# The shared expert's products and the first two expert passes in another order, in a mixture-of-experts layer

## The reference, cut to what matters

```python
def swiglu(t, wg, wu, wd):
    return (jax.nn.silu(t @ wg) * (t @ wu)) @ wd

def moe_ffn(h, ...):                       # T = 512 tokens, D = 1024
    scores = jax.nn.sigmoid(t @ w_router)  # 64 experts, group-limited top 8
    ...                                    # tokens sorted by expert, blocks of one expert
    def expert_block(args):
        tok, wb, e = args
        yb = swiglu(t_pad[tok], w_e_gate[e], w_e_up[e], w_e_down[e])
        return yb * wb[:, None]
    routed = jax.ops.segment_sum(...)      # added back to the tokens' rows
    shared = swiglu(t, w_sh_gate, w_sh_up, w_sh_down)
    return routed + shared
```

## Time and profile before

| | us |
|---|---|
| median of 3 runs | 1037.86 |
| lowest and highest | 1037.82, 1041.65 |
| the profiled execution | 1042.4 |
| its span | 1040.6 |
| TensorE busy in it | 944.7 (91%) |
| DVE, ACT, POOL busy | 513.2, 330.9, 400.1 |
| mean granted TensorE clock | 0.964 |

### The profile page before, as it was taken

The page is one execution under the profiler, slowest core; times in us unless marked ns, Lnnn a source line. Parts: engine busy times, 40 slices in busy tenths (PEclk is TensorE's granted clock), DMA queues, the critical chain, the costliest instruction groups (busy, mean ns, idle before and its releaser), DMA issues.

```text
span 1040.6 us, 13867 instructions
## 1 busy us (share of the span) xinstructions
PE 944.7 (91%) x3980; PEld 388.6 (37%) x3981; DVE 513.2 (49%) x682; ACT 330.9 (32%) x595; POOL 400.1 (38%) x300
## 2 busy tenths in 40 slices
PE   3999999899999989979999898996999999999760
PEld 0554444466555553323333232332333333333220
DVE  2336876777156954434545344442445455454234
ACT  4212222377345422222232232322222323322232
POOL 0312431000000045553556644554455565555531
PEclk9999999999999999989999999998999999999895
DMA  9955452900314967999989999999999999999837
GB/s 368 350 181 202 167 198 71 363 1 2 122 81 156 356 230 284 394 388 377 382 294 339 397 381 370 373 357 367 387 377 362 352 354 372 370 355 366 308 71 243
DMA packets 63180, 298.29 MB, mean 287 GB/s; under 512 B 15189, under 2 KB 15905, under 8 KB 35121
## 3 DMA queue, kind: packets, MB, share of 16 engines
q1 hardware_dynamic: 42130, 258.01, 63.2%
q0 software_dynamic: 19024, 35.68, 14.2%
q10 hardware_dynamic: 2000, 4.28, 1.1%
HBM read 282.15 MB, written 39.32 MB: 309 GB/s over the span
## 4 chain that ended last, share of the span: by engine, by line
PE 46%; DMA 43%; DVE 4%; SPq 4%; issue 3%; ACT 1%; POOL 0%; ACTq 0%; POOLq 0%; DVEq 0%
DMA wring<-in_w_e_down 33%; PE psum L944 13%; PE psum L1186 10%; DMA wring<-in_w_e_up 5%; PE psum L1198 5%; PE psum L1034 3%; PE psum L981 3%; PE psum L1014 3%; PE psum L1005 2%; DMA ring<-in_w_ada 2%; SPq L451 2%; PE psum L1148 2%; DMA expert_sums<-xres,sidx 2%; SPq L427 1%; PE psum L899 1%
## 5 line engine op out<-in xcount | busy, mean ns | idle before, releaser
L1186 PE MATMUL psum<-wring,xres 128*64 x832 | 379.9, 611 | 35.5 <-DVE cur_g L1613 34.2
L1186 PE MATMUL psum<-cur_g,xres 128*64 128x512 f32 x832 | 379.9, 611 | 0.0
L554 POOL DMA_INDIRECT xg<-h_rows,gidx x216 | 249.6, 1156 | 219.4 <-ACT gidx L801 141.0
L1186 PEld LDWEIGHTS psum<-wring,xres 128*64 128x64 f32 x832 | 112.5, 140 | 258.4 <-issue 253.0
L1198 PE MATMUL psum<-wring,rows 128*64 x424 | 190.6, 592 | 1.9 <-ACT rows L797 1.9
L1198 PE MATMUL psum<-rows 128*64 128x512 f32 x424 | 190.7, 592 | 0.0
L1617 DVE STREAM_TRANSPOSE xres<-xg 128x1024 f32<-128x1024 f32 x53 | 108.5, 2047 | 160.9 <-DMA xg<-h_rows,gidx 158.7
L1613 DVE COPY cur_g<-wring 128x1536 f32 x106 | 125.7, 1228 | 46.3 <-SPq L440 46.3
L561 POOL DMA_INDIRECT expert_sums<-xres,sidx x54 | 95.4, 1767 | 96.9 <-DMA expert_sums<-xres,sidx 85.7
L862 ACT COPY xres<-psum 128x1024 f32<-128x1024 f32 x53 | 53.6, 1012 | 190.4 <-PE psum L1198 103.1
L1186 PEld LDWEIGHTS psum<-cur_g,xres 128*64 128x64 f32 x832 | 112.5, 140 | 0.0
(11 more groups left out here) (241 smaller groups left out, 870.1 us busy)
## 6 DMA issues: line engine op xcount, KB each, us to landing
wring<-in_w_e_gate SPq DMA_DIRECT2D x64, 1024.0 KB, 8.4
wring<-in_w_e_up SPq DMA_DIRECT2D x64, 1024.0 KB, 16.1
wring<-in_w_e_down SPq DMA_DIRECT2D x64, 1024.0 KB, 18.2
ring<-in_w_ada SPq DMA_DIRECT2D x20, 1024.0 KB, 5.1
ring<-in_w_in SPq DMA_DIRECT2D x4, 2048.0 KB, 29.1
heads<-in_w_ada SPq DMA_DIRECT2D x4, 1024.0 KB, 23.3
ring<-in_w_out SPq DMA_DIRECT2D x1, 4096.0 KB, 15.2
xg<-h_rows,gidx POOLq DMA_INDIRECT x216
```

Source lines behind the costliest of these rows:

```text
L554: pool.indirect_dma_start(xg[q][:, 256 * s:256 * s + 256], None, hrows, bass.IndirectOffsetOnAxis(gidx[:, q, s:s + 1].bitcast(U32), 0), bo ...
L1186: last = pe.matmul(pp[2][SUB * g:SUB * g + SUB, 512 * q:512 * q + 2 * F] .rearrange("p (u f) -> p u f", u=2), xT[:, q, k, SUB * g:SUB * g ...
```

## The change

TensorE does all eight products of the fourth gate-up ahead of the slot tables, and the four slot tables follow each other. The shared down product of tile 0 goes behind them, ahead of `quarters`; hidden 2 and down 1 behind `quarters`. Passes 0 and 1 are taken out of the loop. Pass 0's gate-up stands ahead of the shared hidden 3, down 2 and down 3; pass 1 follows these. The down product of the pass that does not exist is dropped, and `s_dn`, `s_ht` and `s_yev` are stepped by one more where the shared expert ends, so that all later counts stay. ACT gets the same order. DVE's hidden product has one more wait. SP's and POOL's instructions are the same.

```diff
--- before.py
+++ after.py
@@ -838,38 +838,51 @@
             shared_silu(2)
             shared_keep(1)
             place_distances(2)
-            shared_rows(0)
             pick_places(2)
             place_distances(3)
             pick_places(3)
+            shared_silu(3)
+            shared_rows(0)
             shared_keep(2)
-            shared_silu(3)
             shared_rows(1)
-            shared_keep(3)
-            shared_rows(2)
-            shared_rows(3)
             act.wait_ge(s_idx, 1)
             act.wait_ge(s_tab, 1)
-            act.sem_inc(s_cdn, FJ)
             nb = act.value_load(ntab[0:1, 0:1], min_val=E, max_val=MAXB - 1)
             pairs = act.snap((nb + 1) // 2)
-            for n in range(1, NT):
-                act.wait_ge(s_sh_st[n], 16)
 
             def keep_y(n, q, scattered):
                 act.wait_ge(s_dn, n)
                 act.wait_ge(s_scat, scattered)
                 act.copy(ysb[:, q], pp[q]).then_inc(s_yev, 1)
 
-            with act.Fori(0, pairs, 2) as i:
+            def open_pass(p, q):
+                gather_index(p + 2, q)
+                w = down_weights(p)
+                act.wait_ge(s_gu, p + (NT + 1))
+                act.activation(sg, pp[2][:, 512 * q:512 * q + F], ACT.Silu).then_inc(s_sil, 1)
+                return w
+
+            def close_pass(p, q, w):
+                keep_y(p + (NT + 1), 1 - q, p * 16 + 16)
+                scatter_index(p - 1, 1 - q)
+                copy_down(*w)
+
+            w = open_pass(0, 0)
+            shared_keep(3)
+            shared_rows(2)
+            shared_rows(3)
+            act.sem_inc(s_cdn, FJ)
+            for n in range(1, NT):
+                act.wait_ge(s_sh_st[n], 16)
+            act.sem_inc(s_yev, 1)
+            scatter_index(-1, 1)
+            copy_down(*w)
+            w = open_pass(1, 1)
+            close_pass(1, 1, w)
+            with act.Fori(2, pairs, 2) as i:
                 for q in range(2):
-                    gather_index(i + (q + 2), q)
-                    e, w0 = down_weights(i + q)
-                    act.wait_ge(s_gu, i + (q + NT + 1))
-                    act.activation(sg, pp[2][:, 512 * q:512 * q + F], ACT.Silu).then_inc(s_sil, 1)
-                    keep_y(i + (q + NT + 1), 1 - q, i * 16 + (16 * q + 16))
-                    scatter_index(i + (q - 1), 1 - q)
-                    copy_down(e, w0)
+                    w = open_pass(i + q, q)
+                    close_pass(i + q, q, w)
             turns = act.snap((pairs + 1) // 2)
             n_down = act.snap(turns * 2 + (NT + 1))
             n_scattered = act.snap(turns * 32 + 16)
@@ -1155,7 +1168,7 @@
                     pe.wait_ge(s_hte, n)
                 for j in range(FJ):
                     last = pe.transpose(pp[1][:, 512 + j * P:512 + (j + 1) * P], hmid_sh[:, j:F:FJ], ident)
-                last.then_inc(s_ht, 1)
+                last.then_inc(s_ht, 2 if n == NT - 1 else 1)
 
             def shared_down(n):
                 pe.wait_ge(s_hte, n + 1)
@@ -1170,7 +1183,7 @@
                     for j in range(FJ):
                         last = pe.matmul(o[:, 512 * m:512 * m + 512], hT_sh[:, n % 2, j, :],
                                          w[:, j, 512 * m:512 * m + 512], start=(j == 0), stop=(j == FJ - 1))
-                last.then_inc(s_dn, 1)
+                last.then_inc(s_dn, 2 if n == NT - 1 else 1)
 
             def weights_of(p):
                 e = pe.value_load(tab[0:1, bass.ds(p * 2 + 2, 1)], min_val=0, max_val=E - 1)
@@ -1218,38 +1231,48 @@
             ranks()
             shared_gate_up(2, range(3, KD))
             shared_hidden(1)
-            shared_down(0)
-            shared_gate_up(3, range(0, 3))
+            shared_gate_up(3, range(KD))
             slot_table(0)
-            shared_gate_up(3, range(3, 4))
-            shared_hidden(2)
             slot_table(1)
             slot_table(2)
             table_rows()
             slot_table(3)
-            shared_gate_up(3, range(4, 5))
+            shared_down(0)
             quarters()
-            shared_gate_up(3, range(5, KD))
+            shared_hidden(2)
             shared_down(1)
-            shared_down(2)
-            shared_hidden(3)
-            shared_down(3)
             pe.wait_ge(s_tab, 1)
             nb = pe.value_load(ntab[0:1, 0:1], min_val=E, max_val=MAXB - 1)
             pairs = pe.snap((nb + 1) // 2)
+
+            def open_pass(p, q, w):
+                pe.wait_ge(s_xte, p + 1)
+                pe.wait_ge(s_w, w[0] + 2)
+                gate_up(p, q, w[1])
+
+            def full_pass(p, q, before, w):
+                pe.wait_ge(s_hm, p + NT)
+                turn_hidden(1 - q)
+                open_pass(p, q, w)
+                pe.wait_ge(s_hte, p + NT)
+                pe.wait_ge(s_yev, p + (NT - 1))
+                down(p * 2 + 1, 1 - q, *before)
+
+            w0 = weights_of(0)
+            pe.wait_ge(s_hm, NT)
+            open_pass(0, 0, w0)
+            shared_hidden(3)
+            shared_down(2)
+            shared_down(3)
+            w1 = weights_of(1)
             pe.wait_ge(s_yev, NT - 1)
-            with pe.Fori(0, pairs, 2) as i:
-                for q in range(2):
-                    before = (e, w0) if q else weights_of(i - 1)
-                    e, w0 = weights_of(i + q)
-                    pe.wait_ge(s_hm, i + (q + NT))
-                    turn_hidden(1 - q)
-                    pe.wait_ge(s_xte, i + (q + 1))
-                    pe.wait_ge(s_w, e + 2)
-                    gate_up(i + q, q, w0)
-                    pe.wait_ge(s_hte, i + (q + NT))
-                    pe.wait_ge(s_yev, i + (q + NT - 1))
-                    down(i * 2 + (2 * q + 1), 1 - q, *before)
+            full_pass(1, 1, w0, w1)
+            with pe.Fori(2, pairs, 2) as i:
+                before = weights_of(i - 1)
+                w = weights_of(i)
+                full_pass(i, 0, before, w)
+                w1 = weights_of(i + 1)
+                full_pass(i + 1, 1, w, w1)
             turns = pe.snap((pairs + 1) // 2)
             n_down = pe.snap(turns * 2 + NT)
             pe.wait_ge(s_hm, n_down)
@@ -1628,6 +1651,7 @@
                     e, w0 = gate_up_weights(i + (q + 1))
                     turn_block(1 - q, i * 32 + 64 * (q + 1))
                     dve.wait_ge(s_sil, i + (q + NT + 1))
+                    dve.wait_ge(s_ht, i + (q + NT))
                     dve.scalar_tensor_tensor(hmid, sg, slot_w[:, bass.ds(i + q, 1)],
                                              pp[2][:, 512 * q + F:512 * q + 2 * F], ALU.mult, ALU.mult)\
                        .then_inc(s_hm, 1)
```

## The result

| | before | changed |
|---|---|---|
| median, us | 1039.76 (4 runs) | 1053.62 (4 runs) |
| lowest and highest | 1037.82, 1043.42 | 1051.07, 1058.41 |
| profiled execution, span | 1042.4, 1040.6 | 1051.07, 1048.7 |

A forecast was written before the change was run, and what follows sets the result against it. The weight stream was taken to bound up to 462, then TensorE, then weights again. TensorE's +7.05 and the stream's +7.5 at pass 6's gate-up gave +7.5 us: 1045.4 median, 1049.9 profiled, range 1039 to 1053.

The forecast's parts named there:

- Slot tables, quarters, pass 0: Ahead of the loop: quarters 1.9 us later at 374.7, pass 0 2.6 us earlier at 386.6, its gate-up 1.96 us longer.
- The store: Tile 3's shared rows, behind down 3: stored at 404.1, landing 5.7 us later (bounds 2.6 and 9.0), at 409.8.
- Down 0: Pass 0's down product, waiting for ACT's copy of its weights behind the store: ends near 414.4.
- Gather 2: POOL's first loop work: starts at 411.7, last part lands after 7.27 us at 423.0; pass 2 starts at 426.7.
- TensorE's sum: Pass behind pass on TensorE to the end of pass 6's gate-up: 479.2 against 472.15, +7.05 us.
- The stream: Weight loads up to pass 6: 5.4 + 1 + 1 us dry, 2.75 for two stores, less 0.7: +9.5 us.
- The step that failed: At pass 6's gate-up both chains end together, the larger decides, and nothing differs behind 480: +7.5 us.
- TensorE waits between 480 and 570: Sign that the forecast is wrong: it would mean the weight stream lost more than TensorE did.
- A: No slow clock, store landing in 2.6 us: about +1 us, 1039, within 0.5%; chance 0.17.
- C: Removed empty down and turn are the gain, stream never dry: about -4 us, 1034, at most -6.5; chance 0.08.
- Rival B: Everything at the upper bound, gather 0 landing in 7.5 us and the store in 9.0: +14.8 us, 1052.7; chance 0.13.

The follow-up runs named there:

- both edits and TensorE kept busy: Changed kernel with gather 2 ahead of the store waits, tile 3's shared rows in another buffer, and 32 unread products ahead of pass 0: 1.0031 to before.
- slot-table part: Kernel before with only the fourth gate-up whole ahead of the slot tables and down 0 between tables and quarters: 0.9985 to before.
- whole, both: Changed kernel with gather 2 ahead of the store waits and tile 3's shared rows in another buffer, freeing ACT's copy: 1.0056 to before.
- ACT's copy freed: Changed kernel with tile 3's shared rows in the second gather buffer, so ACT copies pass 0's down weights without waiting for a shared store: 1.0135 to before.
- quarters first and gather 2 early: Changed kernel, both downs and hidden 3 back ahead of pass 0, down 0 behind quarters, gather 2 ahead of the store waits: 0.9989 to before.

## Why the prediction was wrong in size and right in kind

Times of the trace of after have 1.6 us added here.

- **Slot tables, quarters, pass 0.** Quarters at 374.8 (forecast 374.7); pass 0 at 387.5 (386.6); its gate-up 8.74 instead of 7.09. Right, and that the idle time makes the slow start was shown by keeping TensorE busy.
- **The store.** Issued at 404.6 (404.1), but it landed 8.2 us later where I took 5.7. In nine of the ten traces whose store stands among those loads it took 7.9 to 8.4, in the tenth (both edits and TensorE kept busy) 11.3. The 9.0 of the earlier trace rows, with 3 MiB outstanding, was the like row; I had taken the nearest in time. The rule of the Trainium skill weighed in the prediction ("DMA: Bandwidth & Descriptors", "Queues, rings and completion order", packets by turns) would have given about 4 us by my estimate, and these traces do not bear that estimate out.
- **Down 0.** Forecast to end near 414.4, it ended at 419.9. ACT's copy behind the store was in the sum, but with the store 2.5 us too short, and with down 0 itself at 3.4 us. Behind the wait of 3.79 it took 5.35. This moved down load 7 from 414.4 to 419.9.
- **Gather 2.** POOL's first indirect DMA came 3.4 us later than forecast (415.1 against 411.7). I let the gather land 7.27 us behind its last part; it took 2.1 (417.48 to 419.6), with the DMA engines nearly idle (share 0.21). This error of 5.2 us ran against the others: pass 2 at 424.7 (426.7), and the wait ahead of it 3.77 us where I had over 9. Small waits ahead of passes 3 and 6 that I did not have brought pass 6's gate-up to 478.9 (479.2). That TensorE's sum came out right is luck: its terms missed in opposite ways.
- **The stream.** Here the terms do not cancel. I had 1 us dry near 414 and 5.4 ahead of down load 9; it was some 6 us at 410 to 420, and next to none ahead of load 9. The sum came out near all the same: 8.05 - 1.4 = 6.7 us more dry time than before, where I had 7.4 in all. The gate-up loads 12 to 15 landed 7.7 to 10.1 us later than before, against a forecast of 9.5 for the stream.
- **The step that failed:** "Both chains end together, and the larger decides: +7.5 us. Behind 480 nothing differs but the three indices of the loop." The stream's own sum was +9.5. The 2 us between the two are the slow start that pass 6 no longer had. TensorE gained them, the stream of weights did not, and I carried TensorE's figure to the end of the kernel. At pass 17 the weights decide again, before and after:

```profile
589.54 0.78 PE L1186 MATMUL psum<-wring,xres 128*64 x1 [4.65 <-DVE cur_g L1613]
```

```profile
597.44 1.11 PE L1199 MATMUL psum<-wring,xres 128*64 x1 [6.27 <-DVE cur_g L1636]
```

| trace, us | `ranks` to the end of pass 6's gate-up | from there to the end of pass 17's | from there to the end of the span |
|---|---|---|---|
| before | 122.6 | 126.2 | 442.3 |
| slot-table part | 121.2 | 126.3 | 442.2 |
| whole, gather 2 ahead of the store waits | 132.7 | 125.8 | 439.6 |
| whole, both | 125.8 | 126.4 | 445.0 |
| whole | 129.3 | 128.9 | 442.5 |
| whole, again | 129.7 | 128.8 | 439.6 |
| only the passes ahead of the loop | 129.9 | 129.2 | 442.2 |

Up to pass 6 the last three are 6.7, 7.1 and 7.3 us later than before, as TensorE's sum said. Up to pass 17 they are 9.5, 9.7 and 10.3 us later, as the stream's sum said. In the first four rows pass 6 waited 2.8 to 7.2 us for weights and its gate-up was slow (8.7 to 9.4 us), in the last three it took 7.09. All fourteen traces fall apart in this way: the middle column is 125.6 to 126.4 in the six with a slow pass 6 and 128.8 to 129.6 in the eight without. The landings say the same: against before, the gate-up loads 18 to 21 came 10.6 to 11.2 us late in the first trace of the changed kernel, and the loads 24 to 26, which stand behind a stretch in which the full ring holds up SP, 9.4 to 9.5. The time that this stretch left the DMA engines dry, from 530 to 575, fell from 5.0 to 2.3 us; it was the stream's reserve. All this is read from traces; no run changes this one thing alone. The prediction had named its sign, "TensorE waits between 480 and 570": the trace of after has two short ones ahead of pass 17, 0.8 us in all, where before has none.
- **What stays open.** The forecast of +7.5 is short of these traces by 2.0 to 2.8 us, and of the medians (+13.9 and +13.0) by more. The other 3 to 4 us are in none of the traces: behind pass 17 the changed kernel takes no longer than before. There is only one trace of before, its span (1040.6) lies 3.5 us above the median span of 17 later runs (1037.1), and I had put the same shift on the median as on it. Against the slot-table part, whose trace is near its median, the passes alone are 8.7 us late at pass 6 and 11.5 at pass 17, but 1.2 us of these 11.5 are the gain of the slot-table part against before.

Rivals A and C are refuted: the store took 8.2 us, pass 0 started slowly, and the stream ran dry. Rival B came nearest in number (1052.7), but only half by its mechanism: the store came near its 9.0, while gather 0, which it let land in 7.5 us, was being transposed 2.9 us after its last part was issued (380.44 to 383.31). The central claim, that the last shared store holds up the first passes and through them the stream, is shown by the two edits together; neither showed it alone. Putting the shared downs back ahead of pass 0 takes the whole cost away. What remains with both and the clock, 1.0031, I ascribe to the two shared downs less the empty one (3.4 us) and the two stores in the full stretch; that was not taken apart. ACT's longer waits for scatters behind 480 (28.0 to 45.4 us between 478 and 562 in the eight traces without a slow pass 6, 14.8 to 24.8 in the others) go with the 2.8 us more in that stretch; that they cause them is not shown. The cost does not need them: with gather 2 ahead of the store waits they were 18.5 us and the ratio 1.0128.

## What to carry to other kernels

When one event releases two chains that both end in the same queue of transfers, removing one may show nothing, and its trace shows the stall in place or moved (here from 415 to 435); try both together before dropping the theory. Work hidden under a wait is free only there: the shared downs cost nothing under gather 0, and moved behind it they delayed a store that everything else stood behind. Where two chains end together, a saving that only one of them has is not a saving at the end: ask which of them decides at the next wait. For a stream that is nearly the limit, sum its dry time over the whole run, the late reserve too, and read a change of 1% from several executions, not from two profiles.

## What the runs showed of the hardware that I had not expected

Transfers of one size landed after very different times, by what else was in flight: a 512 KB store took 2.6 us with no weight load beside it and 7.9 to 8.4 us (once 11.3) beside 3 MiB of loads. The last part of gather 2 was in use 2.1 us after its issue on nearly idle DMA engines (share 0.21), and 6.7 us (with ACT's copy freed) and 7.3 us (before) on full ones. So a term read from a busy stretch must not be carried into a sum that itself makes the stretch idle. And a wait of TensorE as short as 3.8 us was followed by slow products (down 0 took 5.35 us instead of 3.60, granted clock 0.81 and 0.85), while waits of 1.3 to 1.5 us were not the earlier trace rows. The line is not a matter of the wait alone: with both downs and hidden 3 back, a wait of 2.59 us ahead of pass 4 was followed by a gate-up of 8.8 us (granted clock 0.50 from 431 to 434); in the kernel with quarters first and gather 2 early, a wait of 2.85 us ahead of the same pass was followed by one of 7.1 us (1.00).
